# One expert table made by two sets of slot products, and a weight split moved behind the first tile's rows

## The reference

```
g_prob = softmax(t @ rg_w + rg_b);  g_sel = argmax(g_prob)          # one of 4 groups
e_prob = softmax(logits of the 4 experts in that group)
top_v, top_i = top_k(e_prob, 2);  top_v = top_v / sum(top_v)        # two of them
gate = one_hot(g_sel) * p_g * w_e                                   # a gate per token and expert
y += (silu(t @ w_gate[e]) * (t @ w_up[e]) * gate) @ w_down[e]       # for each expert e
```

## Time and profile before

| | us |
|---|---|
| median of three executions | 1202.74 (1202.72 to 1203.9) |
| the profiled execution | 1204.96 |
| its span | 1203.1 |
| TensorE products busy | 1142.5 (95%) |
| VectorE busy | 999.5 (83%) |
| ScalarE busy | 739.2 (61%) |
| GpSimd busy | 118.5 (10%) |
| mean granted TensorE clock | 0.987 |

### The profile page before, as it was taken

The page is one execution under the profiler, slowest core; times in us unless marked ns, Lnnn a source line. Parts: engine busy times, 40 slices in busy tenths (PEclk is TensorE's granted clock), DMA queues, the critical chain, the costliest instruction groups (busy, mean ns, idle before and its releaser), DMA issues.

```text
span 1203.1 us, 17704 instructions
## 1 busy us (share of the span) xinstructions
PE 1142.5 (95%) x5852; PEld 912.9 (76%) x5852; DVE 999.5 (83%) x1548; ACT 739.2 (61%) x1052; POOL 118.5 (10%) x156
## 2 busy tenths in 40 slices
PE   5999998999999999999889999999999999999994
PEld 4876885787788888888778678757787888888883
DVE  4997996437799999999769889863569999999996
ACT  5234238433788888888542341683338888888883
POOL 5100000001011111110400000000001111111031
PEclk9999999999999999999899999999989999999998
DMA  9722211128999999999854132102399999999976
GB/s 297 277 98 87 81 35 43 53 89 287 325 392 392 393 393 392 394 393 363 202 185 123 53 105 70 37 19 88 134 337 340 391 393 391 393 392 392 391 257 176
DMA packets 145564, 290.35 MB, mean 241 GB/s; under 512 B 17104, under 2 KB 19216, under 8 KB 145472
## 3 DMA queue, kind: packets, MB, share of 16 engines
q1 hardware_dynamic: 130176, 237.63, 55.2%
q0 software_dynamic: 15296, 51.56, 12.9%
HBM read 263.43 MB, written 25.69 MB: 240 GB/s over the span
## 4 chain that ended last, share of the span: by engine, by line
PE 71%; DVE 7%; ACT 3%; issue 2%; DMA 0%; ACTq 0%; DVEq 0%
PE ps L387 20%; PE ps L389 20%; PE ps L388 20%; PE ps L748 2%; DVE w_lo L379 2%; PE ps L606 2%; PE ps L767 1%; PE ps L870 1%; PE ps L856 1%; PE ps L833 1%; DVE x_sb L1389 1%; PE ps L880 1%; ACT w_hi L375 1%; PE ps L708 1%; PE ps L617 1%
## 5 line engine op out<-in xcount | busy, mean ns | idle before, releaser
L387 PE MATMUL ps<-w_hi,a_hi 128*128 128x512 f32 x960 | 381.3, 397 | 12.1 <-DVE w_lo L379 11.2
L375 ACT ACTIVATE w_hi<-raw 128x1024 fp32r<-128x1024 f32 (+1 forms) x256 | 267.6, 1053 | 183.5 <-PE ps L389 178.8
L389 PE MATMUL ps<-w_hi,a_lo 128*128 128x512 f32 x960 | 375.5, 391 | 0.0
L388 PE MATMUL ps<-w_lo,a_hi 128*128 128x512 f32 x960 | 375.0, 391 | 0.0
L379 DVE TENSOR_TENSOR w_lo<-raw,w_hi 128x1024 fp32r<-128x1024 f32 (+1 forms) x256 | 302.2, 1209 | 56.4 <-ACT w_hi L375 48.4
L379 DVE TENSOR_TENSOR w_lo<-arena,w_hi 128x1024 fp32r<-128x1024 f32 x192 | 227.5, 1221 | 8.7 <-ACT w_hi L375 0.4
L375 ACT ACTIVATE w_hi<-arena 128x1024 fp32r<-128x1024 f32 x192 | 203.6, 1063 | 42.7 <-PE ps L389 38.0
L387 PEld LDWEIGHTS ps<-w_hi,a_hi 128*128 128x128 f32 x960 | 181.0, 189 | 50.6 <-issue 11.7
L389 PEld LDWEIGHTS ps<-w_hi,a_lo 128*128 128x128 f32 x960 | 180.8, 188 | 38.4
L388 PEld LDWEIGHTS ps<-w_lo,a_hi 128*128 128x128 f32 x960 | 181.2, 189 | 35.6
L387 PE MATMUL ps<-a_hi,w_hi 128*128 128x512 f32 (+1 forms) x304 | 121.4, 399 | 4.7 <-DVE a_lo L1413 3.4
(11 more groups left out here) (229 smaller groups left out, 1154.9 us busy)
## 6 DMA issues: line engine op xcount, KB each, us to landing
arena<-in_w_down SPq DMA_DIRECT2D x144, 256.0 KB, 8.9
raw<-in_w_gate SPq DMA_DIRECT2D x136, 256.0 KB, 6.6
raw<-in_w_up SPq DMA_DIRECT2D x136, 256.0 KB, 8.3
arena<-in_w_gate SPq DMA_DIRECT2D x120, 256.0 KB, 7.9
arena<-in_w_up SPq DMA_DIRECT2D x120, 256.0 KB, 8.5
raw<-in_w_down SPq DMA_DIRECT2D x112, 256.0 KB, 9.4
raw<-in_w_in SPq DMA_DIRECT2D x80, 256.0 KB, 4.8
y_rows<-arena POOLq DMA_DIRECT2D x42, 256.0 KB, 5.9
```

The lines of the kernel that those rows point to most:

```text
L375: nc.scalar.activation(split_slot(w_hi, n, w), place(S, i, n, w), ACT.Copy).then_inc(S.w_hi_set, 1)
L387: nc.tensor.matmul(o, lh, rh, start=start, stop=False)
L388: nc.tensor.matmul(o, lh, rl, start=False, stop=False)
L389: return nc.tensor.matmul(o, ll, rh, start=False, stop=stop)
```

## The change

The slot products are made in two sets. The first multiplies the 8 one-hot matrices with the token numbers alone (16 columns, bank 3), the second with the gates alone (16 columns, bank 5). Between the two stand 6 `spin` steps, behind the second 14; before there were 17 behind the one set. The second set waits for a ninth `hot_set` per layer, which DVE gives when the gates' values are written.

On DVE only the token values are made between L1509 and the wait for the places. The expert numbers come behind `slots`. The table's token numbers are copied out as soon as the first set is done, with the counts right behind them, and then the gates are worked out. `gslot` is copied out in the middle of `extras`, ahead of the scan, with a wait for the second set (`slot_gates`).

The split of weight piece 11 by DVE goes from before the first tile's rows to behind them. ACT waits for `ovx_set` before the loop over the tiles and no longer behind it.

```diff
+HOT_SETS = 9
@@ TensorE, router
                 for q in range(TT * TOPE):
-                    pe.wait_ge(hot_set, TT * TOPE * l + q + 1)
-                    mm = T.matmul(ps[:, 3, 0:2 * E], slot_hot[:, q, :], R["hot"][:, q, :], start=(q == 0), stop=(q == TT * TOPE - 1))
+                    pe.wait_ge(hot_set, HOT_SETS * l + q + 1)
+                    mm = T.matmul(ps[:, 3, 0:E], slot_hot[:, q, :], R["hot"][:, q, 0:E], start=(q == 0), stop=(q == TT * TOPE - 1))
                 mm.then_inc(tab_ready, 1)
-                spin(7, 17)
+                spin(7, 6)
+                pe.wait_ge(hot_set, HOT_SETS * (l + 1))
+                for q in range(TT * TOPE):
+                    mm = T.matmul(ps[:, 5, 0:E], slot_hot[:, q, :], R["hot"][:, q, E:2 * E], start=(q == 0), stop=(q == TT * TOPE - 1))
+                mm.then_inc(tab_ready, 1)
+                spin(7, 14)
                 pe.wait_ge(tab_set, 2 * (l + 1))
@@ ACT
                 tile_at(main, None, te)
                 n += 8
+                sc.wait_ge(ovx_set, l + 1)
...
                 last_y(l, 0, n + PIECES_E * STORED + 8)
-                sc.wait_ge(ovx_set, l + 1)
@@ DVE, route
+                hot = R["hot"].rearrange("p (k t) n -> p k t n", k=TOPE)
+                V.tensor_tensor(hot[:, :, :, 0:E], R["m12"],
+                                cst[:, C_TOK:C_TOK + TT].unsqueeze(1).unsqueeze(3).to_broadcast(by_expert), ALU.mult)
+
+                ve.wait_ge(pos_ready, l + 1)
+                here = ps[:, 2, 0:TT * E].rearrange("p (t e) -> p t e", t=TT).unsqueeze(1).to_broadcast(by_expert)
+                link(V.tensor_tensor(R["tm"], here, R["m12"], ALU.mult))
+                link(V.tensor_reduce(R["p2"], R["tm"], AX, ALU.add))
+                slots()
                 link(V.tensor_tensor(R["tm"], cst[:, C_IOTA:C_IOTA + E].unsqueeze(1).unsqueeze(1).to_broadcast(by_expert),
                                      R["m12"], ALU.mult))
-                link(V.tensor_reduce(R["e2"], R["tm"], AX, ALU.add))
+                V.tensor_reduce(R["e2"], R["tm"], AX, ALU.add)
+                ve.wait_ge(tab_ready, 2 * l + 1)
+                V.tensor_copy(tab[:, 0:E], ps[:, 3, 0:E]).then_inc(tab_set, 1)
+                V.tensor_copy(R["count"], ps[:, 2, TT * E:(TT + 1) * E]).then_inc(tab_set, 1)
+
                 ve.wait_ge(exp_out, 2 * l + 2)
                 link(V.tensor_reduce(R["gs"], R["ge"], AX, ALU.add))
                 link(V.scalar_tensor_tensor(out=R["den"], in0=R["fe"], scalar=1.0, in1=R["gs"], op0=ALU.add, op1=ALU.mult))
                 link(V.reciprocal(gates[:, 0, :], R["den"]))
                 link(V.tensor_tensor(gates[:, 1, :], gates[:, 0, :], R["fe"], ALU.mult))
-                hot = R["hot"].rearrange("p (k t) n -> p k t n", k=TOPE)
-                V.tensor_tensor(hot[:, :, :, 0:E], R["m12"],
...
+                V.tensor_tensor(hot[:, :, :, E:2 * E], R["m12"], gates[:].unsqueeze(3).to_broadcast(by_expert),
+                                ALU.mult).then_inc(hot_set, 1)
+
+            def slot_gates(l):
+
+                ve.wait_ge(tab_ready, 2 * l + 2)
+                V.tensor_copy(gslot[:, 0:E], ps[:, 5, 0:E])
@@ DVE, extras
                 V.tensor_scalar(R["c2"], e2k[:], float(STORED), None, ALU.is_lt)
+                slot_gates(l)
                 link(V.tensor_tensor_scan(R["cum"], cst[:, C_ONE:C_ONE + E], R["ex"], 0.0, ALU.mult, ALU.add))
@@ DVE, the layer
-                for j in range(9, 12):
+                for j in range(9, 11):
                     lo(ve, main, None, n0 + PIECES_IN + j)
                 n = n0 + PIECES_MIX
                 te = E * l
                 tile_xt(main, None, te)
+                lo(ve, main, None, n0 + PIECES_IN + 11)
```

## The result

The changed kernel took 1212.16 us (median of 6 executions, 1211.05 to 1214.19) against 1204.2 us for the kernel before (6 executions beside it, 1202.72 to 1208.15): ratio 1.0057, 95% interval 1.004 to 1.0074. It is slower, and lies above the forecast's range (1200.4 to 1206.8). The profiled execution took 1213.18 us with a span of 1211.4, 8.3 more than before.

The account below looks back on a forecast made before the run. TensorE's products held most of the chain; only the first tile's start could move. Layer 0 -0.47 and layer 1 -1.10 made -1.6, or -0.9 without layer 1's long low clock; middle -1.2 from 1202.74: 1201.5 us, range 1200.4 to 1206.8.

Parts of the forecast that it names:

- The step that failed: Expert stage: the diff touches nothing in TensorE's busy 40 us stretch, so only the first tile's start moves, once per layer.
- The sums of the new routing: In front of each layer's first tile: step times from mask to a_lo, put at 298.82 against 299.29 in layer 0.
- the 0.47 and 1.10: Forecast gains in us at the first expert tile: 0.47 in layer 0, 1.10 in layer 1 at full clock.
- the forecast's 0.80: Layer 0, slots and first products: copy of token numbers starts at 291.25 instead of 292.05, a gain of 0.80 us.
- Rival B: Behind the slot products: low clock meets 56 records, not 34; slower, sum +3.0 us, 1205.7; chance 0.30.
- forecast 1.1: Slower case's loss in layer 0, in us, with TensorE's clock low until 294.60 as before.
- the 6.8 I took: Layer 1, behind the sparse slot products: low clock for 6.8 us, until 888.50, as profiled before; loss 1.9 us.
- Rival C: First tile's gather lands when it landed, its DMA engines full; layer 0 gains 0; 1202.1 to 1202.7; chance 0.12.
- D: Both layers: more gain than counted, from clock kept up or removed work worth more; -2.5 us and beyond; chance 0.06.
- The split's place: Piece 11's split behind the first tile's rows costs nothing, VectorE idling 2.90 us there; left, a_lo starts at 299.9.
- the expert numbers under VectorE's idle time: Between slots and token copy: 0.6 us of work where VectorE idled about 1 us, cost nothing; without that cover 0.6.
- ACT's earlier wait: ACT's wait for `ovx_set`, earlier in its program but still after it has come: costs nothing.

## Why the prediction was wrong

**The step that failed** is in the first paragraph: nothing that the diff touches lies in the expert stage, "so the change can only move the start of the first expert tile". It also lengthened TensorE's program, and with it moved the code of every later stage. At one place, behind layer 1's taken branch, that put a block's end 22 instructions behind the target. None of the rivals had it. Shown by three kernels without the new routing or with another count (ratios 1.0041, 1.0051, 1.0085), with the stop at the 11th, the 11th and the 1st product, and by the absence of the stall in the ten others. It costs 6.7 us of the profiled 8.3, and 5.1 in the kernel before with nothing but its code moved. Without it the ratios are 0.9996 to 1.0018 (the kernel with 100 instructions aside, which has its own).

The Trainium skill ("Runtime: NRT & Kernel Launch", "Instruction fetch mechanics") says that code is fetched in blocks of 16 KB, ahead and in sequence, that this is mostly hidden, and that a taken branch whose target isn't at hand has to wait for it. The traces agree on the block, and on the wait for the target (a gap of 3.0 us before, 3.1 after). They do not agree that the step to the following block is hidden: behind the branch of layer 1 its packet started 6.3 to 7.6 us after the target's, in all fourteen traces (5.0 to 7.5 in layer 0). That costs where 22 instructions or fewer are left in the target's block; with 70, the fewest of the kernels without a stall (the one with 8 steps), there is no stall, and between the two nothing was tried.

**The sums of the new routing** were right, for a clock at full. The clearest trace is layer 1 of the kernel after with 60 instructions, where the granted clock was 1.00 throughout (mask at 878.25). TensorE's timeline, one window, and VectorE's timeline:

```profile
880.84 1.96 PE L731 MATMUL ps<-arena 128*128 128x16 f32 x16
882.65 1.58 PE L607 MATMUL ps<-cst 128*128 128x128 f32 x12
884.15 1.96 PE L736 MATMUL ps<-arena 128*128 128x16 f32 x16
885.96 3.37 PE L607 MATMUL ps<-cst 128*128 128x128 f32 x28
889.17 1.04 PE L756 MATMUL ps<-cst,arena 128*128 128x128 f32 x8
```

```profile
883.00:886.40 3.40, 3.40 (x32) 3.29 (x31) 2.00 (x14) 0.00 (x0) 1.99 (x2) 1.00 1.04 366
```

```profile
882.84 0.17 DVE L1534 CAST tab<-ps 128x16 int32<-128x16 f32 x1 [0.16 <-PE ps L731]
886.15 0.18 DVE L1548 COPY gslot<-ps 128x16 f32<-128x16 f32 x1 [1.16 <-PE ps L736]
890.44 1.29 DVE L1623 TENSOR_TENSOR a_lo<-ps,a_hi 128x512 fp32r<-128x512 f32 x2 [0.30 <-ACT a_hi L1090]
```

| us behind the mask | forecast | measured, clock full |
|---|---|---|
| first product of the first set | 2.60 | 2.59 |
| token numbers copied | 4.65 | 4.59 |
| second set starts | 5.96 | 5.90 |
| `gslot` copied | 8.02 | 7.90 |
| transposes | 10.9 | 10.92 |
| a_lo | 12.22 | 12.19 |

A record of 16 columns starts every (1.96 - 0.28) / 15 = 0.112 us, where I took 0.115 from wider ones.

**What they were held against** was wrong. The forecast subtracted them from 12.69 and 13.32, the kernel before with a low stretch in each layer, as if only the old kernel had one. The old routing with a full clock, in layer 0 of the moved kernel before, has a_lo 12.13 us behind the mask, its transposes held by the gather until 10.84 (mask and transposes):

```profile
286.46 0.23 DVE L1513 TENSOR_TENSOR arena<-arena 128x64 f32<-128x64 f32 x1
297.30 1.06 PE L750 MATMUL ps<-cst,arena 128*128 128x128 f32 x8 [1.88 <-DMA arena<-h_rows,tab]
```

So with the clock full in both the change gains nothing (12.19 against 12.13), and the 0.47 and 1.10 were the clock's. The earlier token copy is real (4.59 against 5.12 at a full clock; the rest of the forecast's 0.80 was the clock's too), but TensorE's 56 records end only at 10.9.

**Rival B** was right as a mechanism. In the changed kernel the low stretch met the longer queue in both layers: 0.95 lost in layer 0 (forecast 1.1) and 0.37 in layer 1, where it had 3.4 us of it and not the 6.8 I took. At its longest, in the kernel with 20 instructions, it cost 4.2. A low stretch behind the slots comes and goes in either routing: with the two sets and 14 filler steps four of ten layers in the traces had one, with the old single set six of ten. What the longer queue costs in the ratio is not settled. The two runs with 14 filler steps and no stall of several us stand at 1.0014 and 1.0018, those with fewer at 0.9996 to 1.0008, and the intervals overlap. Besides, in these two the branch of layer 0 was 2.6 to 2.8 us shorter than in the changed kernel, of which TensorE lost 2.0 and 1.5 again, waiting for VectorE among the sums behind them. Some 1 to 2 us are likely, not shown.

**Rival C** stays half open. In the nine kernels with two sets, the copy at 4.59 to 4.85, the gather landed 9.71 to 12.31 us behind the mask, 10.77 in the mean of 18 layers; in the five with one set, the copy at 5.12 to 5.68, 10.29 to 11.77, 11.10 in the mean of ten. So an earlier issue brought some 0.3 us and not 0.80, less than the landings vary; in layer 1 of the changed kernel the gather took 7.27 us and landed 0.09 before the transposes. **D** did not come. The split's place, the expert numbers under VectorE's idle time and ACT's earlier wait cost nothing, as forecast: a_lo waited 0.31 for ACT in the changed kernel, not for a split.

The Trainium skill ("TensorE: Matmul & The Clock Gate", Part 1) says that the monitor behind the clock does not restart with the kernel. No run here shows that by itself, but the traces agree with what follows from it: the six executions of the changed kernel had mean granted clocks of 0.984 to 0.988, and of the two layers in one program the one had 3.4 us of low clock behind the slots and the other none (the kernel with 60 instructions), or 10.2 and none (with 20). One trace's low stretch is no property of the kernel, and should not have been in the baseline of a sum.

## What to carry to other kernels

Where a program has a taken branch, count the instructions between its target and the end of its block of 256: any edit that adds or removes instructions ahead of it, fillers and satisfied waits too, moves that distance, and may cost or give back more than the edit itself. Before a small edit is judged, move the code alone by as many instructions and time that. And compare two schedules at the same clock: a sum that subtracts an undisturbed forecast from a disturbed trace has the disturbance as its gain.

## What the runs showed of the hardware

- TensorE's code comes in packets of 16 KB on a queue of its own. Behind the taken branch of layer 1 the next one started 6.3 to 7.6 us after the target's, behind that of layer 0 5.0 to 7.5 us. In the two windows shown of the kernel after, the results' scatters and gathers took 96 to 100% of the 16 DMA engines; whether the load is what makes it late was not tried.
- TensorE goes on 1.4 to 1.6 us after the packet has landed (1.3 to 1.7 behind a branch). When the target's packet starts varies more, 1.0 to 4.1 us after the branch began. A run of 100 instructions without work stopped it for 6.74 us with no branch in between.
- Each such gap may cost twice: in the profile after, 4.17 us of standing still were followed by a granted clock of 0.50 for 6.8 us, in which a product took 0.43 us and not 0.23.
- What shortened the branch of layer 0 from 6.4 to 3.4 to 3.9 us in three of the kernels stays open.
